# Mixer 1's heads: buffers of GpSimd's own, two weight rests made among the heads' squares, convolution banks scaled first, a shorter reciprocal root

## What is computed

```python
def rms_norm(x, w):
    y = x * lax.rsqrt(jnp.mean(x * x, axis=-1, keepdims=True) + EPS)
    return y * w

def hybrid_mixer(h, cos, sin, ...):            # "mixer 1"
    c_q, c_kv, k_rope, conv_in, gate_logits = split(h @ w_in)
    q  = rms_norm(c_q, q_a_norm) @ w_uq        # 8 heads x (64 + 32)
    kv = rms_norm(c_kv, kv_a_norm) @ w_ukv     # 8 heads x (64 + 64)
    q_nope, k_nope = rms_norm(q_nope, ..), rms_norm(k_nope, ..)     # per head
    q_rope = apply_rope(rms_norm(q_rope, ..), cos, sin)
    k_rope = apply_rope(rms_norm(k_rope, ..), cos, sin)
    o_attn = causal_mla_attention(q_nope, q_rope, k_nope, k_rope, v)
    xv, gate_b, gate_c = split(conv_in)
    o_conv = gate_b * causal_conv3(gate_c * xv)
    merged = sum(sigmoid(gate_logits) * (branches @ w_branch))
    return merged @ w_out
```

## Time and profile before

| | |
|---|---|
| median of 3 runs | 1021.87 us (1020.94 to 1022.57) |
| profiled execution, its own time | 1022.38 us |
| its span, first to last instruction | 1020.6 us |
| TensorE busy | 984.7 us, 96% |
| VectorE busy | 780.7 us, 76% |
| ScalarE busy | 535.6 us, 52% |
| GpSimd busy | 10.6 us, 1% |
| mean granted TensorE clock | 0.994 |

### The profile page before, as it was taken

One profiled execution on the slowest core, in us unless ns is written; L12 is line 12 of the kernel. 1 busy time (PEld: TensorE's weight loads), 2 busy tenths in 40 slices (PEclk: granted clock), 3 DMA queues, 4 the chain that ended last, 5 costly groups with the idle time before them and its releaser, 6 DMA issues.

```text
span 1020.6 us, 17346 instructions
## 1 busy us (share of the span) xinstructions
PE 984.7 (96%) x7016; PEld 918.1 (90%) x7016; DVE 780.7 (76%) x1447; ACT 535.6 (52%) x937; POOL 10.6 (1%) x32
## 2 busy tenths in 40 slices
PE   5999999998888999999999999999999999999996
PEld 4999998998887999999998988789999988988895
DVE  6999999978985787685877588656778877577665
ACT  4455554436476555353555545665555555355453
POOL 0000000004000000000000000000000000000000
PEclk9999999999999999999999999999999999999998
DMA  8996998854573555768764445354354555555421
GB/s 331 351 346 261 358 344 329 314 188 159 193 261 125 192 188 188 256 217 200 264 249 165 167 164 192 139 162 148 128 204 164 176 190 203 190 182 171 180 104 41
DMA packets 33277, 213.92 MB, mean 210 GB/s; under 512 B 3757, under 2 KB 6189, under 8 KB 8494
## 3 DMA queue, kind: packets, MB, share of 16 engines
q1 hardware_dynamic: 32910, 211.78, 58.7%
q10 hardware_dynamic: 288, 1.05, 0.3%
HBM read 210.19 MB, written 2.62 MB: 209 GB/s over the span
## 4 chain that ended last, share of the span: by engine, by line
PE 86%; DVE 7%; ACT 3%; issue 1%; POOL 1%; DMA 1%; DVEq 0%; ACTq 0%; POOLq 0%
PE bank L216 84%; DVE sb_ring L195 2%; PE bank L219 2%; ACT sb_ring L192 1%; ACT sb_tmp L192 1%; DVE sb_tq L195 1%; DVE sb_tmp L201 1%; ACT R L192 1%; DVE sb_tmp L195 1%; DVE sb_junk L204 1%; DMA sb_x<-xt 0%; DMA sb_raw<-wts 0%; DVE sb_nst L195 0%; DVE sb_tmp L198 0%; DVE R L195 0%
## 5 line engine op out<-in xcount | busy, mean ns | idle before, releaser
L216 PE MATMUL bank<-sb_h,sb_ring 128*128 128x258 f32 (+2 forms) x3776 | 497.5, 292 | 9.6 <-DVE sb_h L201 3.9
L216 PEld LDWEIGHTS bank<-sb_h,sb_ring 128*128 128x128 f32 x3776 | 476.0, 190 | 24.7 <-issue 5.9
L195 DVE TENSOR_TENSOR sb_ring<-sb_raw,sb_ring 128x1024 fp32r<-128x1024 f32 (+1 forms) x324 | 385.1, 1205 | 2.8 <-ACT sb_ring L192 2.8
L192 ACT ACTIVATE sb_ring<-sb_raw 128x1024 fp32r<-128x1024 f32 (+1 forms) x324 | 320.4, 1038 | 79.1 <-DMA sb_raw<-wts 46.0
L216 PE MATMUL bank<-R_512r,sb_ring 128*128 128x256 f32 (+1 forms) x1608 | 225.3, 301 | 0.0
L216 PEld LDWEIGHTS bank<-R_512r,sb_ring 128*128 128x128 f32 x1608 | 211.3, 188 | 11.9 <-issue 0.3
L216 PE MATMUL bank<-sb_ring,sb_h 128*128 128x512 f32 (+1 forms) x504 | 112.5, 378 | 0.0
L216 PEld LDWEIGHTS bank<-sb_ring,sb_h 128*128 128x128 f32 x504 | 87.4, 188 | 16.6
L204 DVE CUSTOM_DVE_ANT_0 sb_junk<-sb_raw,sb_csil,sb_cols 128x1024 bf16<-128x1024 f32 x72 | 92.3, 1282 | 1.8
L216 PE MATMUL bank<-R_1024r,sb_ring 128*128 128x512 f32 (+1 forms) x576 | 91.6, 320 | 0.0
L216 PEld LDWEIGHTS bank<-R_1024r,sb_ring 128*128 128x128 f32 x576 | 82.0, 188 | 8.2
(11 more groups left out here) (161 smaller groups left out, 560.4 us busy)
## 6 DMA issues: line engine op xcount, KB each, us to landing
sb_raw<-wts SPq DMA_DIRECT2D x193, 1024.0 KB, 4.9
sb_raw<-wts SPq DMA_DIRECT2D x3, 512.0 KB, 3.5
scratch<-R SPq DMA_DIRECT2D x1, 1536.0 KB
sb_x<-xt ACTq DMA_DIRECT2D x2, 512.0 KB, 5.0
out<-R SPq DMA_DIRECT2D x2, 512.0 KB, 2.6
R<-scratch SPq DMA_DIRECT2D x2, 508.0 KB, 9.0
sb_raw<-wts SPq DMA_DIRECT2D x1, 768.0 KB, 4.3
sb_raw<-wts SPq DMA_DIRECT2D x1, 640.0 KB, 4.0
```

Of the source, the lines that this page charges most:

```text
L192: return Issued(self.e and self.e.activation(o, i, func, **kw))
L195: return Issued(self.e and self.e.tensor_tensor(*a))
L216: return Issued(self.e and self.e.matmul(o, w, m, start=start, stop=stop, skip_group_check=True))
```

## The change

- GpSimd's `c_factors` gets small buffers of its own, `sb_cst` (three times six columns) and `sb_krt` (two times 32), in place of VectorE's statistics and of the two `sb_tmp`. Its instructions are the same.
- `head_sums` no longer waits for `nf`; `head_factors` does, at the place where it multiplies by it, and no longer waits for `kr_rope`.
- The heads' steps stand in another order: all four squares of the queries first, a `fill()`, the sums, another `fill()`, then the keys' squares and sums; ScalarE's `v_out` comes last.
- `conv_in` and `conv_out`: VectorE scales both banks as soon as the products are there, and ScalarE copies each shift column behind that; the bank is free after ScalarE's copy. `conv_gate` is split in the scaling and the gating (`conv_gated`), and in `conv_out` both scalings come first.
- `rsqrt` on VectorE: one Newton step and one step of third order in place of three Newton steps, eight instructions in the chain instead of ten; the constant factor that it leaves in its result, `Z_SCALE`, is another.

```diff
@@ -19,7 +19,7 @@
-Z_SCALE = -8192.0
+Z_SCALE = -256.0 / 3.0
...
         self.smx = sb("smx", [128, 4, 8])
+        self.cst = sb("cst", [128, 3, 6])
+        self.krt = [sb(f"krt{i}", [128, 32])[:, :] for i in range(2)]
         self.rt = sb("rt", [128, 4, 2, 32])
...
             self.add("c_sums_out", b, kn)
             done(b, ("c_sums_out",))
-            ab = tmp.take(), tmp.take()
-            self.add("c_factors", kn, ko, ab)
+            self.add("c_factors", kn, ko)
             done(kn, ("kr_rope",))
-            done(ab[0], ("kr_rope",))
-            done(ab[1], ("kr_rope",))
             return ko
...
         def conv_in(i, between):
             banks = project(("conv_in", i), [128, 128], between)
             zx, zc, xs, y = m.zb.take(), m.zb.take(), tq.take(), tmp.take()
-            self.add("conv_shift", i, banks, (zx, zc))
             self.add("conv_x", i, banks[0], xs)
-            done(banks[0], ("conv_x", i))
+            self.add("conv_c", i, banks[1], y)
+            self.add("conv_shift", i, 0, banks[0], zx)
+            done(banks[0], ("conv_shift", i, 0))
             self.add("conv_xs", i, xs, zx)
             done(zx, ("conv_xs", i))
-            self.add("conv_c", i, banks[1], y)
-            done(banks[1], ("conv_c", i))
+            self.add("conv_shift", i, 1, banks[1], zc)
+            done(banks[1], ("conv_shift", i, 1))
             self.fill()
             self.add("conv", i, xs, zc, y)
             done(xs, ("conv_u", i))
@@ -823,10 +823,12 @@
         def conv_out(i, between):
             banks = project(("conv_out", i), [128, 128], between)
             for n in range(2):
+                self.add("conv_gate", i, n, banks[n], ys[i + n])
+            for n in range(2):
                 zb, y = m.zb.take(), ys[i + n]
                 self.add("conv_gate_shift", i, n, banks[n], zb)
-                self.add("conv_gate", i, n, banks[n], zb, y)
-                done(banks[n], ("conv_gate", i + n))
+                done(banks[n], ("conv_gate_shift", i + n))
+                self.add("conv_gated", i + n, zb, y)
                 done(zb, ("conv_gated", i + n))
                 self.add("conv_hi", i + n, y)
                 self.fill()
...
         self.mm(1024, "keys", kn, v_b)
+        own = [(n, t, tmp.take()) for n, t in ((0, 0), (0, 1), (1, 0))]
+        for n, t, b in own:
+            self.add("head_squares", n, t, b, False)
+        b = tmp.take()
+        self.add("head_squares", 1, 1, b, True)
+        self.fill()
+        for n, t, b in own + [(1, 1, b)]:
+            self.add("head_sums", n, t, b)
+            done(b, ("head_sums", n, t))
+        for t in range(2):
+            self.add("k_out", t, kn[t])
+            done(kn[t], ("k_out", t))
+        self.fill()
+        for t in range(2):
+            b = tmp.take()
+            self.add("head_squares", 2, t, b, True)
+            self.add("head_sums", 2, t, b)
+            done(b, ("head_sums", 2, t))
         for t in range(2):
             self.add("v_out", t, v_b[t])
             done(v_b[t], ("v_out", t))
-            self.add("k_out", t, kn[t])
-            done(kn[t], ("k_out", t))
-        for n in range(3):
-            for t in range(2):
-                b = tmp.take()
-                on_act = (n, t) not in ((0, 0), (0, 1), (1, 0))
-                self.add("head_squares", n, t, b, on_act)
-                self.add("head_sums", n, t, b)
-                done(b, ("head_sums", n, t))
         self.add("head_factors")
...
-    def conv_shift(self, i, banks, zbs):
-        e = self.e
-        self.turn(*zbs)
-        e.wait_ge(*self.at("project", ("conv_in", i)))
-        for n in range(2):
-            e.activation(zbs[n].ap[:, 0:1], banks[n].ap[:, T:T + 1]).then_inc(
-                *self.up("shift_out", ("conv_shift", i, n)))
+    def conv_shift(self, i, n, bank, zb):
+        e = self.e
+        self.turn(zb)
+        e.wait_ge(*self.at(("conv_x", "conv_c")[n], i))
+        e.activation(zb.ap[:, 0:1], bank.ap[:, T:T + 1]).then_inc(*self.up("shift_out", ("conv_shift", i, n)))
...
     def conv_xs(self, i, xs, zx):
         e = self.e
-        e.wait_ge(*self.at("conv_x", i))
+        e.wait_ge(*self.at("conv_shift", i, 0))
         e.activation(xs.ap, xs.ap, FN.Identity, bias=zx.ap[:, 0:1]).then_inc(*self.up("conv_xs", ("conv_xs", i)))
     def conv_gate_shift(self, i, n, bank, zb):
         e = self.e
         self.turn(zb)
-        e.wait_ge(*self.at("project", ("conv_out", i)))
+        e.wait_ge(*self.at("conv_gate", i + n))
         e.activation(zb.ap[:, 0:1], bank.ap[:, T:T + 1]).then_inc(*self.up("shift_out", ("conv_gate_shift", i + n)))
...
     def rsqrt(self, v, z, a, event):
 
+
         e = self.e
         self.ts(z.bitcast(I32), v.bitcast(I32), -0.5, ALU.mult, 1597463007.0, ALU.add)
-        s = 1.0
-        for n in range(3):
+        for n in range(2):
             e.wait_ge(*self.last())
             self.tt(a, z, z, ALU.mult)
             e.wait_ge(*self.last())
             self.tt(a, a, v, ALU.mult)
             e.wait_ge(*self.last())
-            e.scalar_tensor_tensor(z, a, 3.0 * s * s, z, ALU.subtract, ALU.mult).then_inc(
-                *self.up("vector_own", *([event] if n == 2 else [])))
-            s = -2.0 * s ** 3
-        assert s == Z_SCALE
+            if n == 0:
+                e.scalar_tensor_tensor(z, a, 3.0, z, ALU.subtract, ALU.mult).then_inc(*self.up("vector_own"))
+        e.scalar_tensor_tensor(a, a, 40.0 / 3.0, a, ALU.subtract, ALU.mult).then_inc(*self.up("vector_own"))
+        e.wait_ge(*self.last())
+        e.scalar_tensor_tensor(z, a, 80.0, z, ALU.add, ALU.mult).then_inc(*self.up("vector_own", event))
...
     def conv_x(self, i, bank, xs):
         m, e = self.m, self.e
         self.turn(xs)
-        e.wait_ge(*self.at("conv_shift", i, 0))
+        e.wait_ge(*self.at("project", ("conv_in", i)))
         e.tensor_tensor(xs.ap, bank.ap[:, 0:T], m.rbc, ALU.mult).then_inc(*self.up("conv_x", ("conv_x", i)))
     def conv_c(self, i, bank, y):
         m, e = self.m, self.e
         self.turn(y)
-        e.wait_ge(*self.at("conv_shift", i, 1))
         e.tensor_tensor(y.ap[:, T:2 * T], bank.ap[:, 0:T], m.rbc, ALU.mult).then_inc(*self.up("conv_c", ("conv_c", i)))
...
-    def conv_gate(self, i, n, bank, zb, y):
-        m, e = self.m, self.e
+    def conv_gate(self, i, n, bank, y):
+        m, e = self.m, self.e
+        e.wait_ge(*self.at("conv", i + n))
+        e.wait_ge(*self.at("project", ("conv_out", i)))
+        e.tensor_tensor(y.ap[:, T:2 * T], bank.ap[:, 0:T], m.rbc, ALU.mult).then_inc(
+            *self.up("conv_gate", ("conv_gate", i + n)))
+
+    def conv_gated(self, n, zb, y):
+        e = self.e
         g, yy = y.ap[:, T:2 * T], y.ap[:, 0:T]
-        e.wait_ge(*self.at("conv", i + n))
-        e.wait_ge(*self.at("conv_gate_shift", i + n))
-        e.tensor_tensor(g, bank.ap[:, 0:T], m.rbc, ALU.mult).then_inc(*self.up("conv_gate", ("conv_gate", i + n)))
-        e.wait_ge(*self.last())
+        e.wait_ge(*self.at("conv_gate_shift", n))
         e.scalar_tensor_tensor(yy, g, zb.ap[:, 0:1], yy, ALU.add, ALU.mult).then_inc(
-            *self.up("conv_gated", ("conv_gated", i + n)))
+            *self.up("conv_gated", ("conv_gated", n)))
...
     def head_sums(self, n, t, b):
         m, e = self.m, self.e
         w, c = head_part(m, n, t)[1], 24 * t + 8 * n
-        e.wait_ge(*self.at("nf"))
         e.wait_ge(*self.at("head_squares", n, t))
         e.tensor_reduce(m.st_v[:, c:c + 8], by_head(b.ap[:, 0:8 * w]), AXIS.X, ALU.add).then_inc(
             *self.up("head_sums", ("head_sums", n, t)))
...
         e.wait_ge(*self.last())
         self.tt(v, v, m.kc("invh"), ALU.mult)
         e.wait_ge(*self.last())
+        e.wait_ge(*self.at("nf"))
         for c, n in parts:
             self.ts(v[:, c], v[:, c], m.nf[:, 1, n:n + 1], ALU.mult, EPS, ALU.add)
         e.wait_ge(*self.last())
-        e.wait_ge(*self.at("kr_rope"))
         self.rsqrt(v, z, m.st_a, ("head_rsqrt",))
         e.wait_ge(*self.last())
         for c, n in parts:
...
-    def c_factors(self, kn, ko, ab):
-
-        m, e = self.m, self.e
-        v, z = m.st_v, m.st_z
+    def c_factors(self, kn, ko):
+
+        m, e = self.m, self.e
+        v, z, a = (m.cst[:, i, :] for i in range(3))
...
-        self.rsqrt(v[:, 0:6], z[:, 0:6], m.st_a[:, 0:6], ("c_rsqrt",))
+        self.rsqrt(v, z, a, ("c_rsqrt",))
...
         e.tensor_tensor(m.nf[:, 1, :], m.nf[:, 0, :], m.nf[:, 0, :], ALU.mult).then_inc(*self.up("c_factors", ("nf",)))
-        self.turn(ko, *ab)
+        self.turn(ko)
...
             self.rope(ko.ap[:, 32 * t:32 * t + 32].unsqueeze(1), k, m.rt[:, 2, t, :], m.rt[:, 3, t, :], 1, 16, 1,
-                      ab[0].ap, ab[1].ap, ("kr_rope_in",), ("kr_rope",))
+                      *m.krt, ("kr_rope_in",), ("kr_rope",))
```

(18 more changed lines are left out.)

## The result

The changed kernel takes 1016.21 us, the median of 5 runs (1014.84 to 1018.02), against 1021.87 us: a ratio of 0.994 with a 95% interval of 0.9928 to 0.9952, 5.7 us less. The same program timed again gave 1016.51 us (6 runs) and a ratio of 0.9934 (0.9919 to 0.9949). The forecast was 3.8 us less, with a range that ended at 1016.3 us: the direction was right, the size was not, and the median fell just outside (the second timing lies just inside).

What follows compares the result with a forecast made beforehand. TensorE, busy 984.7 of 1020.6 us, bounds the kernel, with VectorE setting the pace in mixer 1. Start 0.39, mixer 1 2.7 and end 0.68 make 3.8 us: 1021.9 - 3.8 = 1018.1 us, range 1016.3 to 1020.8.

Steps and rivals of the forecast that it cites:

- mixer 1 to the turned heads: Mixer 1: TensorE's waits shrink as VectorE's work comes sooner; 2.7 us, with 2.2 and 3.65 as ends.
- Start and end: Shorter roots on the path: first product 0.39 us earlier; at the end 0.29 and 0.39, together 0.68 us.
- All roots in the middle lie beside TensorE's work and bring nothing: Norm roots between start and end: shortening them was to gain nothing, since TensorE works beside them.
- Both stalls go ... 0.42 + 1.41 = 1.83 us: Mixer 1's heads: VectorE's waits for GpSimd's `nf` and for the buffer `kr_rope` frees vanish, 1.83 us of VectorE's time.
- Scaling first: conv_in 0: VectorE no longer waits for two shift copies of 0.15 us ahead of the scaling, 0.3 us earlier.
- The heads' factors: Heads' root at 48 columns in mixer 1: two steps fewer in the chain make it 0.49 us shorter.
- The rests among the squares: conv_in 2's second rest ends near 245.5, needed at 252.2, so TensorE's wait of 2.85 us goes.
- The bank: conv_out 0's second bank, needed by conv_in 3, is free 1.78 us behind the first scaling, at 256.3 against 259.97.
- The lead stays: Behind the turned heads at 283.50 the waits are the same, so mixer 1's 2.7 us remain.
- GpSimd's late factors: Rival: `nf` comes late at VectorE's factors, moving all behind by 3.4 us to 1021.5 us; 4 in 100.
- ScalarE's shift copies caught behind a pair of weight halves: Rival: banks freed up to 1.99 us later at four pairs, 8.0 us in all, 1026.1 us; 5 in 100.
- the clock's rival: TensorE's lower-clock stretches: one less gives 1016.6 us, 13 in 100; one more 1019.6 us, 13 in 100.

Runs made afterwards that it cites:

- before_third: The kernel before, unchanged, run again for a further trace of where its lower-clock stretches lie; 1022.48 us.
- after_again: The changed kernel itself, unaltered, timed and profiled once more; 1016.51 us, ratio 0.9934.
- conv_old: The changed kernel with the convolutions' old manner: shift copies first, each scaling and its gating together; 1016.99 us, ratio 0.9947.
- no_rests: The changed kernel without the two `fill()` (rests of weights) among the heads' squares; 1016.71 us, ratio 0.9946.
- the parts by themselves: The kernel before with only the new `rsqrt` and its constant, 1020.74 us; and with all the rest of the change, 1018.94 us.
- pool_only: The kernel before with only GpSimd's own buffers and the moved waits for `nf` and `kr_rope`, old order of steps; 1021.71 us, ratio 0.9999.
- late_b: The changed kernel with the heads' second token half 13 tiles later, the keys 2 and the attention 8 tiles later; 1017.38 us.
- the second trace: The kernel before, unchanged, run again for a second trace; 1022.94 us, ratio 1.0002.

## Why the prediction was wrong, step by step

The two traces to compare are `before_third` and `after_again`, which have the same slow stretch behind the attention. The ledger, in us (the program's first product, which waits for the constants' load, starts at 5.77 and at 5.85, so `after_again` is 0.08 late from the outset, which is added back; the terms are rounded, the sum is not made from the rounded ones):

| term | forecast | measured | from |
|---|---|---|---|
| start, first norm's root | 0.39 | 0.4 | first product 18.43 and 18.13, and 0.08 |
| mixer 1's norm root | 0 | 0.4 | latents' sums 231.82 and 231.13: 0.69 + 0.08 - 0.39 |
| mixer 1 to the turned heads | 2.7 | 4.8 | 283.60 and 278.13: 5.47 + 0.08 less the two above |
| late rests in the next layer | 0 | -0.5 | heads 5.5 ahead, at 748 us 4.95 |
| end | 0.68 | 0.7 | ScalarE's last scaling 1016.80 and 1011.18: 5.62 |
| sum | 3.8 | 5.7 | |

- **Start and end** were right in mechanism and size.
- **"All roots in the middle lie beside TensorE's work and bring nothing"** failed. It asked what TensorE did during the root, and not whether VectorE had a pause between the root and the next thing TensorE waits for. There was none, and 0.4 us of the root passed on.
- **"Both stalls go ... 0.42 + 1.41 = 1.83 us"**: the mechanism was right, the first stall was mis-sized. It is 1.82 us, and 3.2 with the second, as soon as TensorE's clock is not low at 232 to 236 us. The row that I rested on was the visible part of a wait for GpSimd; 1.4 us more of it were covered by the slow stretch. The changed kernel waits for neither. This is two thirds of the 2.1 us that the mixer's term was short of.
- **Scaling first**: 0.3 us forecast for conv_in 0, 0.25 measured (first square 0.94 us sooner, of which 0.69 are the roots). What the order saves behind the first scaling was set against the shift copies and given 0.1 us; from there (257.26 and 252.37) to the turned heads the lead grows by 0.58, and `conv_old` puts 0.43 of it down to the order. This term is about 0.5 short.
- **The heads' factors** were to be 0.49 us shorter and are 0.33 (3.94 and 3.61 us; the four multiplications by `nf` take 0.76 instead of 0.64). Against that stand 0.4 us of hops between instructions that go where VectorE's squares and sums stand together, which no term had. Of the 15.67 - 11.72 = 3.95 us between first square and first scaling, 3.22 are the stalls, 0.33 the factors, 0.4 the hops. With this the mixer's 2.1 us are accounted for: 1.4 + 0.5 + 0.4 - 0.2.
- **"The rests among the squares"**: the wait went, as said, the reason given did not hold (`no_rests`).
- **The bank**: 1.78 us behind the first scaling forecast, 254.15 - 252.38 = 1.77 measured. The prediction's 256.3 for it was late by what stood ahead of it. Before conv_out 2 the wait was to be 2.8 us for ScalarE and is 2.35.
- **"The lead stays"** from 284 us on: right through the attention (5.50 us at 308.32), a little optimistic later.
- **The rivals.** GpSimd's late factors did not decide: `nf` stands at 244.66, VectorE wants it at 247.92, a margin of 3.3 us as claimed, but ScalarE already at 245.18 and not at 247, with 0.5 us to spare. No row shows ScalarE's shift copies caught behind a pair of weight halves. Of the clock's rival only the first trace shows "one stretch less", and the median doesn't rest on it.

For the sum, the median's 5.7 us are the ledger's 5.7. That they agree so closely is in part luck: single executions of either kernel spread over 3 us, and the parts by themselves gave 1.6 + 3.3 = 4.9 us.

## What to carry to other kernels

When a wait for a slow side chain is to be removed, size it by the chain's own end against the time at which the waiting engine would be there if all else ran freely, not by the idle time in one trace: here a slow stretch of TensorE covered 1.4 of 1.8 us of it. That end is itself not fixed; the engines beside the chain move it. Look also for who else waits for the same chain, since without reordering the wait only moves on. Where one engine's queue has no pause up to the next thing that the timed engine waits for, every instruction in it counts, whatever the timed engine is doing beside it, and exchanging pieces of it won nothing here beyond the tenths of hops between them.

## What the runs showed of the hardware

- A stretch at the lower granted clock (0.50) costs only what lies behind it uncovered: the ones at 232 to 236, at 254 to 260 and at 262 to 266 us cost 0.0 to 0.2 us at the turned heads, the one behind the attention's wait (1.8 us, 2.1 in `pool_only`, 2.5 in `late_b`) costs 1.4 to 1.6 us in the next two groups of products. The places vary between executions of one program (four traces of the kernel before have three different sets): the wait of 2.85 us at 255 us was followed by one in the second trace (72 products from 255.16 took 10.63 us) and not in the trace of the prediction, with the same length of wait.
- A GpSimd step on six columns takes 0.20 us while VectorE pauses, and also beside its scalings out of a bank (237.23 and 237.50 in the trace of the prediction) and its sums (243.57 and 243.86 in the changed kernel); beside its rests of weights it takes up to 1.14 us. In the changed kernel, where VectorE no longer pauses, the chain to `nf` takes 10.3 us (234.31 to 244.66) instead of 9.0, and nobody waits for it. VectorE's rests beside it are as long as elsewhere, 1.21 to 1.24 us.
